# Experts' tiles moved to starts at multiples of 512 bytes, with token blocks 384 columns apart

## The reference: what is computed

```python
def expert_choice_ffn(x, router_w, wg, wu, wd):
    ...
    aff = jax.nn.softmax((xt @ router_w).astype(jnp.float32), axis=-1)
    cap = max(1, CAPACITY_FACTOR * n // N_EXPERTS)
    gate, idx = lax.top_k(aff.T, cap)
    xe = xt[idx]
    h = jax.nn.silu(jnp.einsum('ecd,edf->ecf', xe, wg)) * jnp.einsum('ecd,edf->ecf', xe, wu)
    ye = jnp.einsum('ecf,efd->ecd', h, wd) * gate[..., None].astype(x.dtype)
    out = jnp.zeros((n, D), x.dtype).at[idx.reshape(-1)].add(ye.reshape(-1, D))
```

## The kernel before

| tile | start before | past a multiple of 512, of 128 | k-blocks, bytes apart | start with the change |
|---|---|---|---|---|
| `w_h` | 27,712 | 64, 64 | 512 | 28,160 |
| `w_l` | 55,872 | 64, 64 | 512 | 56,320 |
| `x_h` | 84,032 | 64, 64 | 1,152 | 84,480 |
| `x_l` | 93,248 | 64, 64 | 1,152 | 96,768 |
| `h_h` | 102,464 | 64, 64 | 1,152 | 109,056 |
| `h_l` | 115,136 | 448, 64 | 1,152 | 125,952 |

## Time and profile before

### The profile page before, as it was taken

The page is one execution under the profiler, slowest core; times in us unless marked ns, Lnnn a source line. Parts: engine busy times, 40 slices in busy tenths (PEclk is TensorE's granted clock), DMA queues, the critical chain, the costliest instruction groups (busy, mean ns, idle before and its releaser), DMA issues.

```text
span 2901.8 us, 44971 instructions
## 1 busy us (share of the span) xinstructions
PE 2608.1 (90%) x16779; PEld 2295.7 (79%) x16779; DVE 1730.4 (60%) x2343; ACT 1133.7 (39%) x1612; POOL 351.1 (12%) x209
## 2 busy tenths in 40 slices
PE   6997689991999369999999999999999999999990
PEld 4443345551888369999999999999999999999990
DVE  4499736786333666656656656556556556556543
ACT  4100274443222124444444444444444444444433
POOL 0017222221000000110110110110110101101100
PEclk9998899995999579999999999999999999999995
DMA  5000021113544036756766666667667568567538
GB/s 166 15 22 7 0 82 33 32 53 118 171 147 152 29 111 184 202 153 179 196 161 185 178 168 190 165 171 200 160 167 211 149 172 218 139 187 208 149 101 276
DMA packets 620280, 406.82 MB, mean 140 GB/s; under 512 B 16240, under 2 KB 595056, under 8 KB 619120
## 3 DMA queue, kind: packets, MB, share of 16 engines
q1 hardware_dynamic: 605552, 366.96, 43.9%
q0 software_dynamic: 14592, 37.76, 5.8%
HBM read 348.04 MB, written 56.62 MB: 139 GB/s over the span
## 4 chain that ended last, share of the span: by engine, by line
PE 81%; DVE 11%; ACT 2%; issue 2%; DMA 2%; POOL 0%; DVEq 0%; ACTq 0%; SPq 0%; POOLq 0%
PE ps L1172 39%; PE ps L1189 19%; PE ps L964 8%; DVE rows L1289 7%; PE ps L1034 7%; PE ps L918 1%; DMA y<-fin_y 1%; PE ps L939 1%; PE ps L1051 1%; PE ps L1148 1%; PE ps L1139 1%; PE ps L952 1%; ACT rows L785 1%; PE ps L1126 0%; DVE fin_y L1221 0%
## 5 line engine op out<-in xcount | busy, mean ns | idle before, releaser
L1172 PE MATMUL ps<-x_h,w_l 128*128 128x288 f32 x2816 | 835.8, 297 | 3.5 <-issue 3.5
L1172 PE MATMUL ps<-x_l,w_h 128*128 128x288 f32 x2816 | 830.7, 295 | 0.0
L1172 PE MATMUL ps<-x_h,w_h 128*128 128x288 f32 x2816 | 827.9, 294 | 0.0
L1506 DVE TENSOR_TENSOR w_l<-raw,w_h 128x1024 fp32r<-128x1024 f32 (+1 forms) x480 | 639.5, 1333 | 279.1 <-ACT w_h L853 276.6
L853 ACT ACTIVATE w_h<-raw 128x1024 fp32r<-128x1024 f32 (+1 forms) x480 | 547.8, 1145 | 236.2 <-PE ps L1172 227.2
L1172 PEld LDWEIGHTS ps<-x_h,w_l 128*128 128x128 f32 x2816 | 527.5, 187 | 7.0 <-issue 7.0
L1172 PEld LDWEIGHTS ps<-x_h,w_h 128*128 128x128 f32 x2816 | 530.3, 188 | 0.0
L1172 PEld LDWEIGHTS ps<-x_l,w_h 128*128 128x128 f32 x2816 | 528.6, 188 | 0.0
L1189 PE MATMUL ps<-h_h,w_l 128*128 128x288 f32 x1408 | 425.0, 302 | 0.0
L1189 PE MATMUL ps<-h_h,w_h 128*128 128x288 f32 x1408 | 416.5, 296 | 0.0
L1189 PE MATMUL ps<-h_l,w_h 128*128 128x288 f32 x1408 | 415.5, 295 | 0.0
(11 more groups left out here) (224 smaller groups left out, 2714.8 us busy)
## 6 DMA issues: line engine op xcount, KB each, us to landing
raw<-w_gate SPq DMA_DIRECT2D x176, 512.0 KB, 4.3
raw<-w_up SPq DMA_DIRECT2D x176, 512.0 KB, 4.0
raw<-w_down SPq DMA_DIRECT2D x128, 704.0 KB, 6.1
n_x<-x SPq DMA_DIRECT2D x18, 512.0 KB, 4.0
mix_in<-mixed SPq DMA_DIRECT2D x18, 512.0 KB, 4.9
s_x<-x SPq DMA_DIRECT2D x18, 512.0 KB, 5.5
resid<-s_r SPq DMA_DIRECT2D x18, 512.0 KB, 3.2
tokens<-s_h SPq DMA_DIRECT2D x18, 512.0 KB, 5.3
```

Of the source, the lines that this page charges most:

```text
L1172: ins = e.matmul(ps[:, bank, 0:SLOTS], lhs(k), rhs[:, k, :], start=m == 1, stop=m == 3 * KD)
L1506: e.tensor_tensor(w_l[:, m % SPLIT, 0:k * P], raw[:, m % RAW, 0:k * P], w_h[:, m % SPLIT, 0:k * P].bitcast(F32), ALU.subtract).then_inc(lo ...
```

## The change

A k-block of tokens and of activations takes 384 columns of storage (1,536 bytes = 3 x 512) instead of 288, of which the first 288 are used; and the experts' region begins at the next multiple of 512. So every k-block of `x_h`, `x_l`, `h_h`, `h_l`, `w_h` and `w_l` begins at a multiple of 512 bytes. The tiles behind them (`gathered` to `onehot`) move up by some 15 KB and still end below `raw`. The instructions of every engine and their order stay as they were, with the same shapes; only addresses differ.

```diff
+PITCH = 384
...
-        s5 = Region(keep.at)
+        s5 = Region(-(-keep.at // 512) * 512)
         w_h = s5.take("w_h", [P, SPLIT, KF * P], F32R)
         w_l = s5.take("w_l", [P, SPLIT, KF * P], F32R)
-        x_h = s5.take("x_h", [P, KD, SLOTS], F32R)
-        x_l = s5.take("x_l", [P, KD, SLOTS], F32R)
-        h_h = s5.take("h_h", [P, KF, SLOTS], F32R)
-        h_l = s5.take("h_l", [P, KF, SLOTS], F32R)
+        x_h = s5.take("x_h", [P, KD, PITCH], F32R)
+        x_l = s5.take("x_l", [P, KD, PITCH], F32R)
+        h_h = s5.take("h_h", [P, KF, PITCH], F32R)
+        h_l = s5.take("h_l", [P, KF, PITCH], F32R)
...
-                        e.activation(h_h[:, j, :], hid[:, j % 2, :], ACT.Copy).then_inc(hh_done, 1)
+                        e.activation(h_h[:, j, 0:SLOTS], hid[:, j % 2, :], ACT.Copy).then_inc(hh_done, 1)
...
-                                ins = e.matmul(ps[:, bank, 0:SLOTS], lhs(k), rhs[:, k, :],
+                                ins = e.matmul(ps[:, bank, 0:SLOTS], lhs(k), rhs[:, k, 0:SLOTS],
                                                start=m == 1, stop=m == 3 * KD)
```

More of the change, by code:

```diff
@@ L1577, in dve_expert @@
                         e.wait_ge(hh_done, HH0 + KF * ex + j + 1)
-                        e.tensor_tensor(h_l[:, j, :], hid[:, j % 2, :], h_h[:, j, :].bitcast(F32),
+                        e.tensor_tensor(h_l[:, j, 0:SLOTS], hid[:, j % 2, :], h_h[:, j, 0:SLOTS].bitcast(F32),
                                         ALU.subtract).then_inc(hl_done, 1)
```

## The result

The median is 2884.11 us (2882.34 to 2884.41, 4 runs) against 2902.57 us of before (4 runs): ratio 0.9935, 95% interval 0.9918 to 0.9953. The change makes the kernel faster by 18.5 us. The forecast was 2901.5, no change, with a range of 2893 to 2952.

The account below looks back on a forecast made before the run. The prediction took PE's matmuls in the experts to bound the kernel. Its terms, 0 ns x 12,672 + 0, summed to 0, so it forecast the median itself, 2901.5 us, with a range of 2893 to 2952.

Parts of the forecast that it names:

- What bounds the kernel: Experts' stage: PE busy 110.85 of 111.28 us per expert, so only matmul time counts, 12,672 times over.
- the 44 us of cover: Per expert, VectorE works 66.89 of 111.28 us, so slower VectorE, ScalarE or DMA costs nothing until 44 us are used.
- its one term: Experts' matmuls: price change from the new addresses, 0 ns x 12,672 = 0 in the likeliest case.
- a modulus of 512 is as good as excluded: Gate and up chunks: equal 133.3 ns distances over all k mean starts modulo 512 do not set the price.
- units of 128 bytes from the start: Experts' moving reads: unaligned starts touch 10 units where 9 would do, 13.3 ns a matmul; chance 0.16.
- The exact fit of 32 columns: Experts' matmuls: one extra 128-byte unit is 32 more columns, 13.3 ns, matching the whole surplus over streaming.
- The witness: Recurrence's gates, with aligned starts: mean 393 ns against 389 in the output projection, taken as showing no gain from alignment.
- Faster: Experts' matmuls lose their surplus: 147 to 169 us, chance 0.16; or about half, 2817 us, chance 0.03.
- Slower by a collision at equal residues: Experts' moving and stationary blocks meet in the same memory part: 4 ns a matmul, 51 us, 2952 us; chance 0.17.
- +4 and -13.3 ns: Bounds per experts' matmul for an aligned start: the recurrence row's 393 against 389, and the whole surplus.
- Nothing on ScalarE, VectorE and DMA: Accesses to moved tiles costed at nothing: even 10% more on VectorE is 6.7 us, under the cover.
- The uncovered operations: First expert's token split and last result: some two dozen operations under half a microsecond; 10% is about 1 us either way.

Follow-up runs that it names:

- s1_offset_scan: Changed kernel with each of the sixteen experts reading moving columns 0 to 384 bytes further on; 131.7 ns a matmul at 0 bytes, 133.3 at 32, 130.0 at 48.
- e1_start_only: Changed kernel with token blocks back at 1,152 bytes apart, only the region's aligned start kept; 2904.2 us, ratio 1.0004 to the kernel before.
- e2_pitch_only: Changed kernel without the aligned region start: blocks 1,536 bytes apart, all starting 64 bytes past a multiple of 512; 2884.4 us, ratio 0.9934 to the kernel before.
- e7_pitch_320: Kernel before with token blocks 320 columns (1,280 bytes) apart instead of 288; 2881.66 us, ratio 0.9927.

## Why the prediction was wrong

1. **What bounds the kernel** was right: all of the change's effect is in the distance of PE's matmuls, 12,672 of them, and the 44 us of cover for the other engines were never touched. So was the sum's form; its one term was not: the 0 ns measured -1.6 in gate and up ((28.90 - 28.55) / 216) and about -1.2 in down ((4.39 - 4.35) / 33).
2. **The step that failed**: "So a modulus of 512 is as good as excluded." It was drawn from equal distances over k. The premise is true and the inference is not. The matmuls run in a rhythm that several of them share, so a block in a poor relation is not dearer than its neighbour: it puts the whole stream into another rhythm. Before, the tokens alternated between the residues 64 and 192 modulo 256 against weights at 64, one good relation (0 bytes, 131.7 ns) and one bad (128 bytes, 133.3), and all of it ran at 133.3. With every block 0 bytes off it runs at 131.7. `s1_offset_scan` shows the price of each relation, `e1_start_only` the alternation at another place (133.3), `e2_pitch_only` and `e7_pitch_320` the constant relation (131.7).
3. **The theory weighed in its place**, units of 128 bytes from the start, was rightly doubted, and `e1_start_only` refutes it. The exact fit of 32 columns was a coincidence of one rhythm; others have 24 or 28 (130.0 and 131.7 ns).
4. **The witness.** "This is the nearest row there is to the kernel after, and it says: no gain". It was aligned in two of three matmuls, and so not in a constant relation. Made constant, its 4 ns over the output projection shrink to nothing in the median and to 2 in the mean. And the output projection, which has the constant relation 0 by the tiles' places, still has 13.7 ns of surplus with 512 columns: these two rows were no measure of the gain at 288.
5. **The rivals.** Faster was held at 0.19 with sizes of 84 to 169 us; it came with 18.5. Slower by a collision at equal residues did not come: equal residues are among the better relations. The price of an aligned start was bounded by +4 and -13.3 ns, and -1.6 lies in that, but the range was cut at 2893 for want of a case of that size. A term whose bounds are known and whose mechanism isn't deserves weight between the bounds.
6. **Nothing on ScalarE, VectorE and DMA**: right, 66.89 and 66.78 us for an expert on VectorE, 49.67 and 49.58 on ScalarE. The uncovered operations were put at under half a microsecond each; 66.89 / 100 and 49.67 / 71 are 0.67 and 0.70, so that the 1 us should have been nearer 2. It changes nothing.

Left open is what in the chip makes the rhythm. The surplus is not in proportion to the stationary columns, nor fixed over moving columns; it is gone at the half clock in the one stretch that shows it, with 512 columns, and it was between 10.0 and 16.6 ns in everything tried with 288 columns. Open too is why steps of 304 and 368 columns differ, and what picks one of two rhythms. Not tried were relations of `x_h` and `x_l` that differ from each other, and the same search for the 512 columns of the output projection.

## What to carry to other kernels

Where a stream of float32r matmuls is the bound, measure the distance from start to start and compare it with the streaming time; if a surplus is left, the place of the moving blocks against the stationary ones is worth a scan. For this shape, 128 x 128 by 288 columns, it paid to keep the step between blocks at a multiple of 256 bytes, so that one relation holds for all of them. Then let each repetition of an unrolled loop read at another offset: one profile prices sixteen of them. Check the best in a whole kernel, since one repetition may have caught one of two rhythms. And don't infer from equal costs within a stream that its members don't differ, when the stream is pipelined.

## What the runs showed of the hardware that was not expected

- A float32r matmul of 288 columns costs 130.0 to 136.6 ns at the same clock, by nothing but its addresses, and with a constant relation the price repeats after 256 bytes (0 and 256, 32 and 288, 96 and 352 bytes).
- Four bytes count: 44 and 48 bytes give 130.0, 52 gives 133.3 ns. The Trainium skill's "SBUF — State Buffer", section "Specifications (TRN2)", has lines of 16 bytes with a penalty for each cross to a new line. By that alone starts at 44, 52 and 84 bytes, which touch 73 such lines each (worked out from that figure), would cost the same; the trace has 130.0, 133.3 and 136.6 ns.
- One layout can run in two rhythms, 130.0 or 132.5 ns, for some hundred matmuls on end, and change at an interruption of under a microsecond (0.86 us in the chain).
